# Expert accumulation on TensorE: one 128x128 product per slot, or four 64x64 tiles over two slots

## What is computed

```python
def peer_ffn(h, w_q, keys1, keys2, u, v):      # cut to what matters
    q = h @ w_q                                # 8 heads x 256
    s1, s2 = q1 @ keys1.T, q2 @ keys2.T        # 128 scores each
    experts, gate = top16 of all sums of the two top16 lists, softmax of the 16
    act = gelu(sum_d(u[experts] * h)) * gate   # one dot product per chosen expert
    return sum over heads and experts of act * v[experts]
```

## Time and profile before

| what | value |
|---|---|
| median of 3 runs | 3274.03 us (3273.01 to 3278.45) |
| the profiled execution: from its first to its last instruction | 3271.5 us |
| TensorE matmul busy | 2675.8 us |
| VectorE busy | 1576.5 us |
| ScalarE busy | 753.7 us |
| POOL busy | 761.2 us |
| first and last dot product of the expert slots | 1472.3 and 3252.8 us |

### The profile page before, as it was taken

One profiled execution on the slowest core, in us unless ns is written; L12 is line 12 of the kernel. 1 busy time (PEld: TensorE's weight loads), 2 busy tenths in 40 slices (PEclk: granted clock), 3 DMA queues, 4 the chain that ended last, 5 costly groups with the idle time before them and its releaser, 6 DMA issues.

```text
span 3271.5 us, 30806 instructions
## 1 busy us (share of the span) xinstructions
PE 2675.8 (82%) x8280; PEld 1393.7 (43%) x8280; DVE 1576.5 (48%) x4013; ACT 753.7 (23%) x1784; POOL 761.2 (23%) x768
## 2 busy tenths in 40 slices
PE   7999999976778689948887788877888778877876
PEld 3444455554367534423443343433444333433332
DVE  2000023014366633236666666666666666666664
ACT  2000111011022231212222322222222222322222
POOL 0000000000000000004444344334444344434443
PEclk8999999997988889969889988889989888988999
DMA  4223223235612273248999899989999899989997
GB/s 191 84 83 118 90 84 125 84 112 192 243 65 90 83 288 131 90 201 364 375 380 394 361 379 373 385 353 397 377 382 400 362 379 394 374 358 376 384 390 314
DMA packets 157280, 867.32 MB, mean 265 GB/s; under 512 B 14690, under 2 KB 52914, under 8 KB 68404
## 3 DMA queue, kind: packets, MB, share of 16 engines
q0 software_dynamic: 99072, 711.64, 53.5%
q1 hardware_dynamic: 58170, 155.21, 13.1%
HBM read 822.12 MB, written 44.67 MB: 265 GB/s over the span
## 4 chain that ended last, share of the span: by engine, by line
PE 17%; DVE 14%; DVEq 8%; issue 7%; DMA 6%; ACT 4%; POOL 1%; ACTq 0%; POOLq 0%; SPq 0%
PE e_acc L1766 14%; DVE e_expert L1545 6%; DMA e_expert<-in_peer_uv,e_num 5%; DVEq L1547 5%; PE e_q L1775 3%; ACT w_head L1673 1%; ACT e_act L1697 1%; DVE e_coef L1556 1%; POOL e_expert L1533 1%; ACT e_diag L1705 1%; DMA e_wq<-in_w_q 1%; DVE e_hot L1607 1%; DVE e_hot L1604 1%; DVE e_number L1609 1%; DVE e_i L1573 1%
## 5 line engine op out<-in xcount | busy, mean ns | idle before, releaser
L1766 PE MATMUL e_acc<-e_expert,e_diag 128*128 128x512 f32 x2560 | 1269.1, 650 | 371.7 <-ACT e_diag L1705 371.7
L1766 PEld LDWEIGHTS e_acc<-e_expert,e_diag 128*128 128x128 f32 x2560 | 516.0, 209 | 1037.4 <-issue 852.9
L1545 DVE CUSTOM_DVE_ANT_0 e_expert<-e_expert,e_xb 128x1024 f32<-128x1024 f32 x640 | 765.9, 1223 | 286.5 <-DMA e_expert<-in_peer_uv,e_num 257.1
L1533 POOL DMA_INDIRECT e_expert<-in_peer_uv,e_num x640 | 708.8, 1108 | 691.4 <-PE e_acc L1766 552.2
L428 PE MATMUL pj<-w_chunk,hT 128*128 128x512 f32 x800 | 345.3, 594 | 0.8 <-ACT small L465 0.8
L1705 ACT ACTIVATE e_diag<-ident,e_coef 128x128 f32<-128x128 f32 x640 | 221.9, 394 | 165.8 <-DVE e_coef L1556 161.7
L1528 POOL COPY e_num<-idx 128x8 uint32 x80 | 25.9, 324 | 918.1 <-DVEq L1620 557.7
L1697 ACT ACTIVATE e_act<-e_dots 128x2 f32<-128x2 f32 x320 | 65.5, 205 | 746.2 <-DVEq L1547 746.2
L428 PEld LDWEIGHTS pj<-w_chunk,hT 128*128 128x128 f32 x800 | 152.5, 191 | 192.2 <-issue 192.2
L445 PE MATMUL pj<-hT,w_chunk 128*128 128x512 f32 x512 | 226.9, 596 | 4.6 <-DVEq L531 3.5
L1775 PEld LDWEIGHTS e_q<-e_h2T,w_head 128*128 128x128 f32 x1280 | 160.0, 197 | 48.5 <-issue 38.2
(11 more groups left out here) (394 smaller groups left out, 2329.0 us busy)
## 6 DMA issues: line engine op xcount, KB each, us to landing
w_chunk<-in_w_big SPq DMA_DIRECT2D x18, 2048.0 KB, 9.0
wm_later<-in_w_mod POOLq DMA_DIRECT2D x8, 2048.0 KB, 8.5
scratch_proj<-chunk_out POOLq DMA_DIRECT2D x10, 1280.0 KB
m_w<-in_w_out SPq DMA_DIRECT2D x3, 4096.0 KB, 22.3
e_expert<-in_peer_uv,e_num POOLq DMA_INDIRECT x640
wm<-in_w_mod SPq DMA_DIRECT2D x4, 2048.0 KB, 18.0
xbcT<-scratch_xbcT SPq DMA_DIRECT2D x8, 1024.0 KB
qkT<-scratch_qkT SPq DMA_DIRECT2D x8, 1024.0 KB, 6.8
```

The source lines that it names most:

```text
L1533: nc.gpsimd.indirect_dma_start(expert[:, j, :], None, dr["peer_uv"], bass.IndirectOffsetOnAxis(num[:, half, j:j + 1], 0)).then_inc(in_slot ...
L1545: nc.vector.tensor_tensor_reduce(expert[:, j, 0:D], expert[:, j, 0:D], xb[:, :], 1.0, 0.0, ALU.mult, ALU.add, dots[:, half, j:j + 1])
L1766: last = nc.tensor.matmul(acc[:, c * 512:(c + 1) * 512], diag[:, j, :], expert[:, j, D + c * 512:D + (c + 1) * 512], start=False, stop=False)
```

## The change

`diag` of a slot becomes 128 x 64: its rows 0 to 63 hold the diagonal of tokens 0 to 63, and its rows 64 to 127 that of tokens 64 to 127, made from a new constant `ident64` (the two column halves of the identity added). A group of two slots is now eight products of 64 rows by 64 columns by 512, instead of four of 128 x 128 x 512. The token half `r` sets the rows of the array and the accumulator `acc[r]`; the slot's place in the group, `col`, sets the columns of the array and the PSUM partitions 64 * col onward. Four such products use the four quarters of the array. Both slots of a group are freed together, behind the last of the eight. At a block's end each accumulator holds the two slots' sums on its two partition halves; ScalarE copies both to SBUF (`halves`) and TensorE folds them with `ident64` into `acc[0]`. The two accumulators take the PSUM room of `sq` (now in SBUF) and of the second query bank.

```diff
@@ channel_mixer, buffers
-        diag, zero = sb("diag", [P, HALF, P]), sb("zero", [P, P])
+        diag, zero = sb("diag", [P, HALF, HP2]), sb("zero", [P, P])
+        halves, sq = sb("halves", [P, 2, D]), sb("sq", [P, D])
-        acc = ctx.enter_context(nc.psum_tensor("e_acc", [P, D], F32))
-        sq = ctx.enter_context(nc.psum_tensor("e_sq", [P, D], F32))
-        qb = [ctx.enter_context(nc.psum_tensor(f"e_q{i}", [P, 512], F32)) for i in range(2)]
+        acc = [ctx.enter_context(nc.psum_tensor(f"e_acc{r}", [P, D], F32)) for r in range(2)]
+        q_bank = ctx.enter_context(nc.psum_tensor("e_q", [P, 512], F32))
+        qb = [q_bank[:, n * P:(n + 1) * P] for n in range(2)]
@@ vector, once
+            nc.vector.tensor_tensor(t["ident64"][:, :], t["ident"][:, 0:HP2], t["ident"][:, HP2:P], ALU.add).then_inc(zero_ready, 1)
@@ scalar, diagonals
-                    last = nc.scalar.mul(diag[:, at, :], t["ident"][:, :], coef[:, half, at:at + 1])
+                    last = nc.scalar.mul(diag[:, at, :], t["ident64"][:, :], coef[:, half, at:at + 1])
@@ scalar, end
                 act.wait_ge(f_mm, b + 1)
+                for r in range(2):
+                    nc.scalar.copy(halves[:, r, :], acc[r][:, :])
+                act.drain()
+                act.sem_inc(halves_ready, 1)
+                act.wait_ge(f_folded, b + 1)
                 act.wait_ge(f_free, b + 1)
-                nc.scalar.copy(f[:, :], acc[:, :])
+                nc.scalar.copy(f[:, :], acc[0][:, :])
@@ tensor, begin (and end alike, with start=False, stop=True)
-                for half in range(2):
-                    nc.tensor.matmul(acc[:, half * 512:(half + 1) * 512], zero[:, :], z512, start=True, stop=False)
+                for r in range(2):
+                    for c in range(2):
+                        nc.tensor.matmul(acc[r][:, c * 512:(c + 1) * 512], zero[:, :], z512, start=True, stop=False)
@@ tensor, group_products
                 for j in range(GROUP * q, GROUP * (q + 1)):
                     pe.wait_ge(in_slot[j], seen * 16 + 16)
-                    for c in range(2):
-                        last = nc.tensor.matmul(acc[:, c * 512:(c + 1) * 512], diag[:, j, :],
-                                                expert[:, j, D + c * 512:D + (c + 1) * 512], start=False, stop=False)
-                    last.then_inc(slot_free, 1)
+                pe.sem_inc(pe_passed, 1)
+                for c in range(2):
+                    for r in range(2):
+                        tokens = slice(HP2 * r, HP2 * (r + 1))
+                        for col in range(2):
+                            j = GROUP * q + col
+                            last = nc.tensor.matmul(acc[r][HP2 * col:HP2 * (col + 1), c * 512:(c + 1) * 512], diag[tokens, j, :],
+                                                    expert[tokens, j, D + c * 512:D + (c + 1) * 512], start=False, stop=False)
+                last.then_inc(slot_free, 2)
@@ tensor, end
                 last.then_inc(f_mm, 1)
+                pe.wait_ge(halves_ready, b + 1)
+                pe.sem_inc(pe_passed, 1)
+                for r in range(2):
+                    for c in range(2):
+                        last = nc.tensor.matmul(acc[0][HP2 * r:HP2 * (r + 1), c * 512:(c + 1) * 512], t["ident64"][:, :],
+                                                halves[:, r, c * 512:(c + 1) * 512], start=True, stop=True)
+                last.then_inc(f_folded, 1)
```

More of the change, by code:

```diff
@@ L1420, in channel_mixer @@
     QUERIES_AT = 1
+    HP2 = P // 2
     with ExitStack() as ctx:
@@ L1454, in channel_mixer @@
         num_ready, zero_ready = sem("num_ready"), sem("zero_ready")
+        halves_ready, f_folded = sem("halves_ready"), sem("f_folded")
         x_copied, x1_in, x_ready, f_mm, f_out, acc_free, f_free, ms_ready, root_ready, ss_ready, y_ready, y_out = (
@@ L1662, in _ @@
         def _(act):
+            act.wait_ge(zero_ready, 2)
             act.sem_inc(acc_free, 1)
@@ L1678, in queries @@
                 for n in range(2):
-                    last = nc.scalar.copy(qT[:, n, :], qb[n][:, 0:P])
+                    last = nc.scalar.copy(qT[:, n, :], qb[n])
                 last.then_inc(q_moved, 1)
@@ L1740, in _ @@
             pe.sem_inc(slot_free, RING)
-            pe.wait_ge(zero_ready, 1)
+            pe.wait_ge(zero_ready, 2)
             z512 = zero[:, :].unsqueeze(1).to_broadcast([P, 4, P])
@@ L1774, in query @@
                 for m in range(KT):
-                    last = nc.tensor.matmul(qb[n][:, 0:P], w_head[:, m, n * P:(n + 1) * P], h2T[:, m, :],
+                    last = nc.tensor.matmul(qb[n], w_head[:, m, n * P:(n + 1) * P], h2T[:, m, :],
                                             start=(m == 0), stop=(m == KT - 1))
@@ L1795, in end @@
             def end(b):
-                for c in range(2):
-                    last = nc.tensor.matmul(acc[:, c * 512:(c + 1) * 512], zero[:, :], z512, start=False, stop=True)
+                for r in range(2):
+                    for c in range(2):
+                        last = nc.tensor.matmul(acc[r][:, c * 512:(c + 1) * 512], zero[:, :], z512, start=False, stop=True)
                 last.then_inc(f_mm, 1)
+                pe.wait_ge(halves_ready, b + 1)
+                pe.sem_inc(pe_passed, 1)
+                for r in range(2):
+                    for c in range(2):
+                        last = nc.tensor.matmul(acc[0][HP2 * r:HP2 * (r + 1), c * 512:(c + 1) * 512], t["ident64"][:, :],
+                                                halves[:, r, c * 512:(c + 1) * 512], start=True, stop=True)
+                last.then_inc(f_folded, 1)
             schedule(pe, prepare, begin, body, end)
@@ L1807, in programme @@
         t.update({n: sb(n, [P, P], BF16) for n in ("ident_16", "maskF_16", "maskB_16")})
+        t["ident64"] = sb("ident64", [P, P // 2])
         t["iota_i"], t["iota"] = sb("iota_i", [P, TOPK], mybir.dt.int32), sb("iota", [P, TOPK])
```

## The result

The changed kernel takes **3284.38 us** (median of 9 runs, 3280.32 to 3289.76), the kernel before 3274.03 (9 runs beside them). The ratio is 1.0028, with a 95% interval of 1.0018 to 1.0038: slower by about 10 us where 84 us of gain were forecast. The profiled execution is 3287.7 us long, 16.2 more than before's.

What follows compares the result with a forecast made beforehand. It took a ring of 8 slots to bind the kernel, with a 4.4 us DMA gap in each head. 3271.5 - 110 (heads) + 26 (block ends) = 3187.5, plus 2.5 for the median: 3190 us, range 3133 to 3224 (8 in 10: 3140 to 3370).

Steps and rivals of the forecast that it cites:

- Four tiles at once: TensorE's expert products: 16 passes take the time of 4, a group 1.71 us at full clock; chance 0.45.
- Both rivals on the array: Expert products: two tiles at a time, group 3.42 us, 3326 us (0.33); or no overlap, 6.83 us, about 3880 (0.12).
- Slot 0 no sooner: First group of a head, at half clock: slot 0 is still freed after the time of 4 passes, 3.4 us.
- At the full rate, and the 1.5 us of weak start are saved: Fetches after a head's gap: bytes still flow from T0+12 (T0: head's first dots), now at full rate, saving 1.5 us.
- weak start: DMA flow after each head's gap comes back at 270 GB/s instead of 426, costing some 1.5 us.
- The 3.24 us wait goes: Before VectorE's gate product: the query ends sooner, so the 3.24 us wait for ScalarE disappears.
- The term of a head: Period of a head: 41.5 us, 2.9 us less than 44.4; over 38 heads 110 us saved (76 to 167).
- The block's end: Extra zero products, copies and fold cost 7.4 us, net 5.2 as the last group ends sooner; five times, 26 us.
- The gain is eaten: Rival: four tiles run, but half clock and drains leave under 1 us saved a head; 3255 to 3285, chance 0.10.
- the first rival: Expert products only two tiles at a time: group 3.42 us, slot 0 free 2.8 us later; 3326 us, chance 0.33.
- its last sentence: Sign of failure: the groups' span does not halve, or it halves and the DMA gap stays as wide.
- the DMA gap: Once in each head the DMA engines run dry, all 8 slots landed and none free; 4.4 us above 40.

Runs made afterwards that it cites:

- b_num: Kernel before, with POOL copying a half's expert numbers without first waiting for slot 0 to be free: 3272.68 us, ratio 0.9989 to the kernel before.
- a_num: Changed kernel, with POOL copying a half's expert numbers without first waiting for slot 0 to be free: 3234.93 us, ratio 0.987 to the kernel before.
- a_nofold: Changed kernel without the copies of the halves and the fold at a block's end, its output incomplete: 3263.76 us, ratio 0.9964 to the kernel before.
- a_cinner: Changed kernel with a group's eight products reordered, both column halves of one tile next to each other: 3286.44 us, ratio 1.0036 to the kernel before.
- the fastest kernel: Changed kernel with early copy of expert numbers, eight zero products behind a head's last group, and no closing zero products: 3172.63 us, ratio 0.9693.

## Why the prediction was wrong

The forecast's mechanism held, its arithmetic of a head didn't.

**Four tiles at once: right.** 5120 records, and the start of a group's first four records is 6 to 7 ns apart (2027.892, 2027.898, 2027.905, 2027.911), that of the next four 0.48 us later, then each 0.43. Both rivals on the array fall: a tile's second pass doesn't hold the next tile, and a group isn't 3.4 or 6.8 us.

**Slot 0 no sooner: right.** POOL goes on with it at T0+7.94 before and T0+7.96 after, on the mean.

**"At the full rate, and the 1.5 us of weak start are saved": this step failed.** It put the weak start down to slots that come free one after another, and so had the last slot land at T0+32. It lands at T0+34.10 and its dots start at T0+34.12. Slot 0's dots come at T0+15.73, not T0+14.5 (12 + 2.5), and slot 1's at 19.13, 3.4 behind slot 0's; from there each slot takes 2.5, and 19.13 + 6 x 2.5 is 34.1. Slot 1 was free 2.6 us sooner, but POOL could issue its fetch only 0.2 us sooner, and it landed no more than 0.1 us sooner (19.10 against 19.17). Nor does a sooner issue of it help: from b_num to a_num it moves from T0+11.17 to T0+9.89, and slot 1 lands at T0+17.33 and T0+17.81. So the weak start isn't made by slots that come free late. For its first 1.2 us I take it to be the first fetch's own latency, which the prediction left out: 4.6 us from the end of the issue to the dots where the bytes take 2.5. The Trainium skill (DMA: Bandwidth & Descriptors, Anatomy of one DMA) gives a DMA of this kind a fixed 2.0 us beside its bytes; the trace agrees, with 2.1 in the head from 2015.94, counted from the end of POOL's issue. The other 0.9 us, which slot 1 loses behind slot 0, have no cause shown. That this landing holds the head, a_num shows: 1.3 us off slot 0's landing took 1.3 off the head.

**"The 3.24 us wait goes": right, and worth half a microsecond.** The longest wait of VectorE for ScalarE fell from 3.6 to 0.9 us. But behind that wait stood the landing of the data: slot 3's dots moved from T0+24.68 to T0+24.12 only. The prediction had the last slot land at T0+33.5, 1.4 us before VectorE took it. By the DMA's semaphore records it landed at T0+34.26 in the head of the earlier trace rows and at T0+34.21 on the mean, 0.4 us before VectorE took it. So the query's wait had 0.4 to 0.5 us to give and not 1.4, and the landing, which was to give 1.5, gave 0.1. The term of a head, 2.9 us, measured 0.52, and 110 us became 18.

**The block's end: right, with luck in one term.** 5.2 us net were forecast five times, 26 us; measured were 5.8 four times and 6.6 once, 30 us. a_nofold gives back 20 of it. The zero products and the copies came as priced (1.8 and 1.93 us against 1.71 and 2.02). The fold was priced at 3.42 us for eight passes one after another at full clock; it took 3.30 with its tiles in pairs and most of it at half clock, two errors that cancel.

**"The gain is eaten" (0.10, 3255 to 3285)** is what came, at the edge of its range, but for another reason than it gave. It had the half clock and drains fall on the chain. The clock did fall, to 0.78, yet curing it helps before (44 us) more than after (33 us), and a_num gains 49 us at a clock of 0.79. The drains don't show on the chain: behind the group at 2027.89 TensorE's weight loads pause for 0.81 us ahead of the query and its products start 0.52 us apart where 0.43 is the pace, and the query still ends 5 us sooner after T0 than before.

One figure of the first rival was off by itself: 8 passes of which 7 at half clock are 6.4 us, so slot 0 would have come 3.0 us later and not 2.8.

Of what was to show the forecast wrong, its last sentence came true: the groups' span halved and the DMA gap stayed as wide.

## What to carry to other kernels

When an engine's saving is to shorten a ring, list every chain that ends at the consumer's next step, with its time after the same starting point, and take the gain up to the second latest only. Here three ended within a microsecond, and taking away two of them gave half a microsecond. Price the restart of a dry DMA queue as a latency of its own, which a faster consumer doesn't touch; an earlier issue does. Slots behind the first that come free sooner shorten that restart only if their fetches then land sooner, which here they didn't. And before work is moved to an idle engine, look at what stands in that engine's queue at that moment.

## What the runs showed of the hardware

Float32 products of 512 columns are two passes each, and four 64x64 tiles overlap all the same, with starts 6 to 7 ns apart. In a_cinner, where two instructions of one tile stand next to each other, the starts in a round are 13 to 14 ns apart and the rounds keep 0.43 us: products for other tiles go ahead of one whose tile is busy. The Trainium skill (TensorE: Matmul & The Clock Gate, Part 3) says that matmuls start and end strictly in program order. In a_cinner the group's time says otherwise, and the measurement decides: by my estimate from the pace of 0.43 us, a group in that order would take ten rounds, 4.3 us, if no instruction started before the one ahead of it, and it takes four. In after whole instructions can still start in their order, and only their second passes wait. The records don't name their tile, so this rests on the times.

The fold's products, 128 rows by 64 columns and 8 passes, take 3.30 us at 2191.45 and 1.95 us at the last block's end (3275.19): pairs of tiles side by side, with rounds 0.85 us apart at half clock (granted 0.50 from 2193 to 2195) and 0.43 us at full clock. And a few zero products in TensorE's idle time were worth 1.3% in the kernel before and 1.0% in the changed one; from 1480 to 3180 the granted clock rose from 0.90 to 0.95 and from 0.78 to 0.85.

What stays open: why the flow needs some 6 us to reach 410 GB/s after a gap although POOL issues one fetch 2.06 us behind the first and the next three each 1.3 to 1.6 us, and so whether the 0.9 us that slot 1 loses beside slot 0 could be had. No run changed how the first fetches are cut. Open too is what the fastest kernel would give with its zero products behind the transposes: in it VectorE's four waits for these are 20.6 us.
